# Two side programs of a feed-forward trade places in each weight slot

## What is computed

```python
for i in range(DEPTH):                       # 2 layers
    proj = h @ w_in[i]
    p_conv, p_swa, p_ret, p_rwkv = split_cols(proj, IN_SIZES)
    y_conv = short_conv_mixer(p_conv, conv_w[i])
    y_swa = swa_mixer(p_swa, ...)            # windowed attention with sinks, chunks of 64
    y_ret = retention_mixer(p_ret, ...)      # state carried over chunks, RMS norm per head
    y_rwkv, v_first = rwkv7_mixer(p_rwkv, ...)   # token-wise state, done in blocks of 64
    mix = concatenate([y_conv, y_swa, y_ret, y_rwkv]) @ w_out[i]
    h = layer_norm(ALPHA * h + mix)
    h = layer_norm(ALPHA * h + conv_glu_ffn(h, ffn_w_up[i], ffn_conv_w[i], ffn_w_down[i]))
```

## Time and profile before

| | |
|---|---|
| median of 3 executions | 3695.01 us |
| lowest and highest | 3693.22, 3697.1 us |
| the profiled execution | 3696.15 us |
| its span (first to last instruction) | 3694.3 us |
| mean granted clock of TensorE | 0.967 |
| TensorE, VectorE, ScalarE, GpSimd busy | 3544.3, 1332.8, 894.6, 41.1 us |

### The profile page before, as it was taken

One profiled execution on the slowest core, in us unless ns is written; L12 is line 12 of the kernel. 1 busy time (PEld: TensorE's weight loads), 2 busy tenths in 40 slices (PEclk: granted clock), 3 DMA queues, 4 the chain that ended last, 5 costly groups with the idle time before them and its releaser, 6 DMA issues.

```text
span 3694.3 us, 52540 instructions
## 1 busy us (share of the span) xinstructions
PE 3544.3 (96%) x22062; PEld 2947.8 (80%) x22062; DVE 1332.8 (36%) x3277; ACT 894.6 (24%) x2726; POOL 41.1 (1%) x76
## 2 busy tenths in 40 slices
PE   6888999999999999999999999999999999999897
PEld 4776787878888788887888878887888878888786
DVE  2323443143441433324443343323444143442441
ACT  4221232032320323113231222212232032320211
POOL 0000000000000000000000000000000000000000
PEclk9968999999999999999999999999999999999998
DMA  4203333443244332443324432344323443344443
GB/s 155 90 1 104 119 97 104 142 135 111 92 127 156 123 109 92 137 145 118 106 95 126 143 120 90 99 137 139 118 92 120 148 133 113 96 134 150 129 154 97
DMA packets 121563, 433.72 MB, mean 117 GB/s; under 512 B 13280, under 2 KB 17504, under 8 KB 121200
## 3 DMA queue, kind: packets, MB, share of 16 engines
q1 hardware_dynamic: 119312, 423.01, 36.4%
q0 software_dynamic: 2016, 7.34, 0.6%
HBM read 426.11 MB, written 4.19 MB: 116 GB/s over the span
## 4 chain that ended last, share of the span: by engine, by line
PE 92%; ACT 4%; DVE 3%; issue 1%; DMA 0%; SPq 0%; POOL 0%; DVEq 0%; ACTq 0%; POOLq 0%
PE psum L747 61%; PE psum L1178 17%; PE psum L741 2%; PE psum L933 1%; PE psum L944 1%; PE psum L942 1%; ACT hT L446 1%; PE psum L1124 1%; PE psum L1120 1%; PE psum L902 1%; PE psum L1060 1%; PE psum L1122 1%; PE psum L1062 1%; PE psum L1105 1%; PE psum L958 1%
## 5 line engine op out<-in xcount | busy, mean ns | idle before, releaser
L747 PE MATMUL psum<-hT,slots 128*128 128x256 f32 (+1 forms) x8832 | 2077.5, 392 | 27.3 <-ACT rstdT L416 7.8
L747 PEld LDWEIGHTS psum<-hT,slots 128*128 128x128 f32 x8832 | 1682.0, 194 | 334.8 <-issue 71.2
L1178 PE MATMUL psum<-gT,slots 128*128 128x256 f32 (+1 forms) x2816 | 619.6, 383 | 0.0
L1178 PEld LDWEIGHTS psum<-gT,slots 128*128 128x128 f32 x2816 | 536.0, 190 | 80.9 <-issue 0.2
L685 ACT ACTIVATE last<-psum 128x2 f32<-128x2 f32 x352 | 60.2, 171 | 1108.4 <-PE psum L747 1108.4
L1250 DVE SCALAR_TENSOR_TENSOR hT<-hT,psum 128x256 f32<-128x256 f32 (+1 forms) x128 | 54.4, 425 | 648.3 <-PE psum L1178 535.0
L1680 DVE TENSOR_SCALAR tmpG<-raw,par 128x256 f32<-128x256 f32 (+1 forms) x176 | 62.5, 355 | 535.9 <-ACT raw L686 535.9
L747 PE MATMUL psum<-mixT,slots 128*128 128x256 f32 (+1 forms) x1024 | 230.8, 386 | 4.9 <-issue 2.5
L747 PEld LDWEIGHTS psum<-mixT,slots 128*128 128x128 f32 x1024 | 194.9, 192 | 39.7 <-issue 10.6
L437 ACT ACTIVATE sqb<-hT 128x256 f32<-128x256 f32 (+1 forms) x128 | 50.8, 419 | 705.4 <-DVE hT L1268 677.9
L1680 DVE TENSOR_SCALAR gT<-raw,par 128x256 f32<-128x256 f32 (+1 forms) x176 | 62.5, 355 | 352.9 <-ACT raw L686 352.8
(11 more groups left out here) (223 smaller groups left out, 3003.5 us busy)
## 6 DMA issues: line engine op xcount, KB each, us to landing
slots<-in_weights SPq DMA_DIRECT2D x792, 512.0 KB, 3.5
out<-prpt POOLq DMA_DIRECT2D x8, 512.0 KB, 3.1
wset<-in_x POOLq DMA_DIRECT2D x6, 512.0 KB, 4.1
tab<-in_tables SPq DMA_DIRECT2D x6, 512.0 KB, 5.0
con<-in_consts SPq DMA_DIRECT2D x1, 1450.0 KB, 11.4
tab<-in_tables SPq DMA_DIRECT2D x2, 544.0 KB, 5.8
wset<-in_x SPq DMA_DIRECT2D x2, 512.0 KB, 4.4
par<-in_params SPq DMA_DIRECT2D x2, 386.5 KB, 5.9
```

The costliest lines, as they stand in the source:

```text
L747: ins = mm(psum[:parts, i % 2, :n], lhsT, rhs, start=k == 0, stop=k == len(pairs) - 1)
L1178: ins = mm(psum[:, i % 2, :n], w[:, e * P:(e + 1) * P], gT[:, k, :n], start=k == 0, stop=k == KF - 1)
```

## The change

In the loop over the units, on ScalarE (L711), TensorE (L1198) and VectorE (L1708), the list of the two sides is turned round. The start-up, GpSimd's and SyncE's programs, and the steps themselves stay as they are.

```diff
@@ -708,7 +708,7 @@
                     if u + 1 == NCH:
                         a.wait_ge(S["in_par"], 32)
                     rest(project(u + 1))
-                    sides = [rwkv(u + 1), chain(side(u + 1), finish_tiles(u - 1))]
+                    sides = [chain(side(u + 1), finish_tiles(u - 1)), rwkv(u + 1)]
```

## The result

The changed kernel takes 3706.94 us (median of 8 executions, 3703.65 to 3712.97); the kernel before, timed beside it, 3695.78 us (3693.22 to 3698.89). The ratio is 1.003, 95% interval 1.0019 to 1.0041: slower by 11.2 us. The profiled execution of after took 3705.32 us with a span of 3703.5, 9.2 us more than before.

A forecast was written before the change was run, and what follows sets the result against it. TensorE, busy 96% of the span, was taken to bound the kernel. Terms of -2.3 (wait), +1.0 (new waits), +3.3 (shapes) and nothing for the clock gave +2.0 us, so 3697 us, range 3689 to 3704 us.

The forecast's parts named there:

- What bounds the kernel: Whole span: TensorE is busy 96%, so an order pays only by taking its idle time or shortening its same work.
- Part 1, the wait: Six two-tile windows, slot 16: TensorE's wait for the exponentials before the attention transposes goes, -2.3 us.
- Rival 4: Slot 16: VectorE's new order makes RWKV late, 5 us, 3702 us; chance counted within the forecast's 0.78.
- Part 2, new waits: TensorE waits anew in slot 10 (0.1 us in seven windows) and slot 31 (0.4 us): +1.0 us in all.
- Part 3, shapes: TensorE in the turned slots: changes between 128x128 and 64-row work cost +0.41 us per two-tile window, +3.3 us in all.
- rival 1: 35 slots with retention or attention directly before RWKV: each shape change costs 0.28 us, +9.8 us, 3707 us; chance 0.08.
- Part 4, the clock: Behind TensorE's long alternating steps: as many half-clock stretches as before, no net cost; chance strays 6.6 us at worst.
- Rival 2: Behind the long alternating steps: five more half-clock stretches at 1.7 us, +8.5 us, 3705 us; chance 0.06.
- theory C2: Follow-up theory: distance between long steps decides falls; with transposes added, 3 to 6 of 14 L1060 steps hit, 3698 to 3704 us.

The follow-up runs named there:

- the padded old order: The kernel before, order unchanged, with eight repeated transposes added in slot 5 of each window (6.1 us in all): 3695.27 us, ratio 0.9998 to before.
- by slot 7: The changed kernel with slot 7 (7 and 11 in the three-tile window) put back in the order of before: 3695.04 us, ratio 1.0001 to before.
- the padded new order: The changed kernel with eight repeated transposes added in slot 5 of each window (6.1 us in all): 3709.62 us, ratio 1.003 to before.

## Why the prediction was wrong

It forecast 3697 us, within 3689 to 3704; 3707 is outside, and the direction had a chance of 0.14. The time in the slots past 33, which it named as a sign, is the same within 0.3 us over the seven feed-forwards.

**What bounds the kernel**: right. TensorE's own time decides, and with it what one slot costs there.

**Part 1, the wait**: right in mechanism and size. The 2.3 us in six windows are gone, slot 16 is 0.58 us shorter, and L595 stands behind the exponentials at no cost to TensorE. Rival 4 didn't come.

**Part 2, new waits**: the one in slot 31 of the three-tile window is 0.47 us, where 0.4 was taken. The 0.1 us in slot 10 of each window didn't come.

**Part 3, shapes**: right in its sum, +0.41 per window, against -0.2 measured and 0.46 of wait taken out, some +0.3; its terms were less right where the long steps are concerned. A slot of transposes costs 0.05 us more on average, as worked out. A flank behind R falls into the next slot, so only the sum of the slots 5, 6, 11 to 14, 19 to 21, 23 and 24 shows it, +0.34 where +0.35 stood with slot 16. Slot by slot it is -0.1 to +0.1. The L1060 step saves 0.20 and not 0.10: the step itself is shorter behind D, 2.80 us in place of 2.91. L1120 costs 0.20 to 0.25, where +0.13 stood. The direct S to R change of rival 1 is free, as taken: in slot 2 both kernels need 5.51 us. The rule of the Trainium skill's page "TensorEngine Tiling (Array Packing)", section "Tiling Modes", counted by changes of mode, gave zero here; the rows' sum was nearer, and no run shows whether each change drains the engine.

**Part 4, the clock**: this is the step that failed. "So I expect as many such stretches, with chance in it" put the term at nothing, and it came to up to 12 us: in the seven windows 102 us are at half clock in place of 78. Two errors led there. First, I took the number of falls for a draw of chance, over which a median would average. There is chance in it, but the two kernels also differ in themselves: 16 and 16, 22 and 22 in two profiles each. I had allowed 6.6 us for it "at worst, less in a median of runs". Second, I took it that the same steps with dense work on both sides would be followed by as many falls wherever they come. Turning the slots moves the step of slot 7 by 0.47 us and the flanks against that of slot 3, and in four windows of after both meet a fall, in before in one. Rival 2 priced the right mechanism (five more stretches, 3705 us) and got 0.06; its "against", that nothing in the work of TensorE grows, was true and didn't help. The mean clock of the windows, which I named as the sign to watch, stayed inside 0.94 to 0.98 as forecast. The sign was badly put: compared window by window it fell in five of seven and shows the loss; the band was too wide for it.

**What stays open.** That a small shift deals the falls anew is shown by the padded old order and by slot 7. What of the shift decides is not shown: the distance to the last long step, that to earlier ones, the time at which a step comes, or the dense work ahead of it. Whether S directly behind D also makes a fall behind L1120 more likely isn't settled: with slots 17 and 22 turned 12 to 14 of 14 are hit, without it 9 to 11. Five kernels with and four without are no proof, since their distances differ too. And I can't foretell for a given change which steps are hit: theory C2 failed in the padded new order.

## What to carry to other kernels

Before two steps trade places on a busy TensorE, look at the granted clock behind each slow step. Then compare the mean clock window by window, or the time at half clock, before and after; a count of falls alone misses how long they last. If such falls are there, a change worth less than a few tenths of a per cent can't be judged by its own merit; take the slow step away first (here by grouping matmuls of one shape, 2%), then try the order. In the grouped kernel the same turn took 0.1% off the time, in the ungrouped one it added 0.3%.

## What the runs showed of the hardware that was not expected

- Where matmuls of 128 and 64 rows alternate, each pair of records takes 0.36 us; 16 records in eight such pairs take 2.80 us, eight of one shape and then eight of the other 1.52 us, with no change to the sums. For 24 records of 16, 64 and 128 rows it is 3.1 in place of 4.3 us.
- Adding 6.1 us of work to the busiest engine left the time where it was (3695.27 against 3695.58 us of before in the same comparison), since less time passed at half clock, in the profiled execution 55 us of the windows in place of 78.
- The half-clock stretches fall behind the same steps in two executions of before, and behind the same but one in two of after, though the spans differ by 1.6 and 1.1 us. Other executions of the same kernels depart from that, by their mean clock and time.
